# State-space stage of a three-block model: decay sums through DRAM, differential norm inside the groups, merge units behind the last group

## The reference, cut to what matters

```
att = (rms_norm_3(att, subln_w[l], SUBLN_EPS) * (1.0 - lam_init)).reshape(b, s, ATT_V_WIDTH)
ssd = ssd_branch(z, xbc, dt_raw, ...)
merged = sigmoid(gate_a) * (att @ w_branch_attn[l]) + sigmoid(gate_s) * (ssd @ w_branch_ssd[l])
x = x + merged @ w_out[l]
```

```
xbc = silu(causal_depthwise_conv(xbc, conv_w, conv_b))
cum = cumsum(ac);  seg = cum_i - cum_j;  decay = exp(where(causal, seg, -inf))
cb = einsum('bign,bjgn->bgij', cc, bc)
y_diag = einsum('bgij,bgrij,bjgrp->bigrp', cb, decay, xc)
...
y = y * silu(z);  y = y * rsqrt(mean(y*y, per group) + eps) * norm_w
```

## Time and profile before

| | us |
|---|---|
| median of 3 runs (3091.27 to 3093.89) | 3092.34 |
| the profiled execution | 3088.23 |
| its span | 3086.4 |
| TensorE busy in it | 2936.3 (95%) |
| VectorE busy | 925.2 (30%) |
| ScalarE busy | 453.8 (15%) |

### The profile page before, as it was taken

The page is one execution under the profiler, slowest core; times in us unless marked ns, Lnnn a source line. Parts: engine busy times, 40 slices in busy tenths (PEclk is TensorE's granted clock), DMA queues, the critical chain, the costliest instruction groups (busy, mean ns, idle before and its releaser), DMA issues. The chain is left out here.

```text
span 3086.4 us, 33957 instructions
## 1 busy us (share of the span) xinstructions
PE 2936.3 (95%) x14263; PEld 2277.3 (74%) x14263; DVE 925.2 (30%) x1969; ACT 453.8 (15%) x855; POOL 0.2 (0%) x4
## 2 busy tenths in 40 slices
PE   7999999999999999998999999999897899999997
PEld 6888788888887888886888877889786434344343
DVE  2117521021053210532025326455202323222222
ACT  1001410010042100222010012244201010010011
POOL 0000000000000000000000000000000000000000
PEclk9999999999999999998999999899998899999999
DMA  7434144444443443533544443344351899999996
GB/s 241 163 124 163 55 149 151 146 158 146 130 123 116 145 156 122 128 106 82 148 152 148 152 116 91 96 123 116 103 153 43 361 425 427 426 426 427 425 427 257
DMA packets 358885, 590.10 MB, mean 191 GB/s; under 512 B 11376, under 2 KB 315120, under 8 KB 336112
## 3 DMA queue, kind: packets, MB, share of 16 engines
q1 hardware_dynamic: 358064, 586.09, 54.0%
q10 hardware_dynamic: 704, 2.32, 0.2%
HBM read 587.33 MB, written 1.05 MB: 191 GB/s over the span
## 5 line engine op out<-in xcount | busy, mean ns | idle before, releaser
L679 PE MATMUL bank<-hR,ring 128*128 128x256 f32 x3520 | 763.5, 380 | 8.5 <-DVE hR L416 5.6
L679 PEld LDWEIGHTS bank<-hR,ring 128*128 128x128 f32 x3520 | 669.5, 190 | 101.6 <-issue 7.1
L815 PE MATMUL bank<-big,ring 128*128 128x256 f32 x2016 | 440.0, 381 | 4.9 <-ACT big L1013 4.3
L815 PEld LDWEIGHTS bank<-big,ring 128*128 128x128 f32 x2016 | 385.4, 191 | 58.8 <-issue 4.7
L2622 PE MATMUL bank<-ring,wk 128*64 128x512 f32 x1408 | 313.2, 597 | 4.7 <-DMA ring<-in_w_expert_gate 4.7
L2622 PEld LDWEIGHTS bank<-ring,wk 128*64 128x64 f32 x1408 | 99.9, 138 | 211.1 <-issue 211.1
L714 DVE TENSOR_TENSOR wk<-bank,rstd 128x512 f32<-128x512 f32 x88 | 60.9, 692 | 484.3 <-PE bank L679 484.0
L2648 PE MATMUL bank<-big,wk 128*64 128x512 f32 x352 | 155.8, 595 | 15.1 <-ACT wk L2674 15.1
L851 DVE SCALAR_TENSOR_TENSOR xT<-bank,xT 128x512 f32<-128x512 f32 x36 | 24.9, 692 | 454.3 <-PE bank L815 454.3
L2711 DVE TENSOR_TENSOR hT<-bank,hT 128x512 f32<-128x512 f32 x92 | 63.6, 691 | 314.7 <-PE bank L2609 312.4
L1807 PE MATMUL bank<-big,ring 128*128 128x256 f32 x640 | 141.0, 379 | 1.5 <-ACTq L2841 1.0
(11 more groups left out here) (376 smaller groups left out, 2777.7 us busy)
## 6 DMA issues: line engine op xcount, KB each, us to landing
ring<-in_ffn_w_in SPq DMA_DIRECT2D x88, 1024.0 KB
ring<-in_w_expert_gate SPq DMA_DIRECT2D x44, 2048.0 KB
ring<-in_w_expert_up SPq DMA_DIRECT2D x44, 2048.0 KB
ring<-in_w_in SPq DMA_DIRECT2D x96, 512.0 KB
big<-in_w_expert_down SPq DMA_DIRECT2D x44, 1024.0 KB
ring<-in_ffn_w_out SPq DMA_DIRECT2D x20, 2048.0 KB
ring<-in_w_up SPq DMA_DIRECT2D x22, 1024.0 KB
hR<-in_w_expert_down SPq DMA_DIRECT2D x22, 1024.0 KB
```

Source lines behind the costliest of these rows:

```text
L679: last = nc.tensor.matmul(k.bank[:, n % 4, h * S:(h + 1) * S], w[:, c, h * 256 + m * P:h * 256 + (m + 1) * P], k.hR[:, c, :], start=c == 0 ...
L815: return nc.tensor.matmul(k.bank[:, 4 + o // 2, (o % 2) * S:(o % 2 + 1) * S], w[:, c, o * P:(o + 1) * P], self.src[:, n, :], start=n == 0 ...
```

## The change

- The 128 instructions of L2184 are gone. `turn` transposes the cumulative sums (32 heads on 32 partitions) once, between parts of `project_x(0)`; ScalarE copies them out and writes them to a DRAM tensor (`take_rows`); then ScalarE issues, for each head of a group, a transfer that reads the head's row of 1 KB to all 128 partitions (`load_rows`, 4 a group, two groups ahead, into two halves of `hR`). VectorE's differences read that copy in place of the PSUM banks.
- `sums` moves behind `project_x(0)`; `cumulate` and `turn` go between its quarters. `spread` is halved and put behind `project_x(2)` and `project_x(3)`, its `variance`, `root`, `inverse` and `apply` into groups 0, 1 and 2.
- In the last group the merge's unit (0, 0) runs where other groups have `project_x(g+1)`; unit (1, 0) runs ahead of `turn_y(7)`; the units of block 0 and 1 are fetched and used in the order (0,0), (1,0), (0,1), (1,1). Gates and branches change places in the banks.
- `Ssd` loses its barrier; TensorE waits for `yt_taken` instead.

```diff
+        if self.per == 2:
+            self.order[0:4] = [(0, 0), (1, 0), (0, 1), (1, 1)]
...
+    def turn(self, pe):
+        k, nc = self.k, self.k.nc
+        pe.wait_ge(self.tail_ready, 1)
+        for t in range(T):
+            last = nc.tensor.transpose(k.bank[0:32, 7, S + t * P:S + (t + 1) * P], k.sd[:, 4 + t, :], k.c("ident"))
+        last.then_inc(self.rows_turned, 1)
...
+    def take_rows(self, act, chain):
+        act.wait_ge(self.rows_turned, 1)
+        rows = self.k.drow[0:32, 0:S]
+        chain(self.k.nc.scalar.activation(rows, self.k.bank[0:32, 7, S:2 * S], ACT.Copy))
+        act.dma_start(self.k.arg["decay_rows"], rows).then_inc(self.rows_kept, 16)
...
-        self.sub.sums(pe)
-        project_x(0)
-        self.dt.cumulate(pe)
-        self.sub.spread(pe)
-        project_z(0)
-        pe.wait_ge(self.sub.applied, 1)
+        project_x(0, {1: self.dt.cumulate, 2: self.dt.turn})
+        self.sub.sums(pe)
+        project_z(0)
         for g in range(self.G):
-
-            if g:
-                pe.wait_ge(self.seg_done, g)
-            for c in range(T):
-                for r in range(self.R):
-                    last = nc.tensor.matmul(k.bank[:, 5 + c, r * P:(r + 1) * P],
-                                            k.sd[:, 2 + c, 4 * g + r:4 * g + r + 1].to_broadcast([P, P]), k.c("le"),
-                                            start=True, stop=True)
-            last.then_inc(self.cum_bc, 1)
-
             pe.wait_ge(self.conv_silu, g + 1)
...
             if g + 1 < self.G:
                 project_x(g + 1)
+            else:
+                pe.wait_ge(self.sub.applied, 2)
+                pe.wait_ge(self.copied, 2 * self.G)
+                self.merge.unit(pe, 0)
+            if g in (1, 2):
+                self.sub.spread(pe, g - 1)
...
-        pe.wait_ge(self.copied, 2 * self.G)
-        self.fill(pe)
+        pe.wait_ge(self.z_silu, self.G)
+        pe.wait_ge(self.y_summed, self.G)
+        self.merge.unit(pe, 1)
         pe.wait_ge(self.yt_taken, self.G - 1)
         turn_y(self.G - 1)
+        pe.wait_ge(self.yt_taken, self.G)
...
+        def load_rows(g):
+            for r in range(self.R):
+                act.dma_start(self.rows(g, r), self.dt.row(4 * g + r).to_broadcast([P, S])).then_inc(self.rows_loaded[g % 2], 16)
...
         self.sub.square(act, chain)
         self.dt.logs(act, chain)
-        self.sub.root(act, chain)
+        self.dt.take_rows(act, chain)
+        self.dt.decay(act, chain)
+        act.wait_ge(self.dt.rows_kept, 16)
+        load_rows(0)
+        load_rows(1)
         act.wait_ge(self.pads_zero, 1)
         copy_in(0)
-        self.dt.decay(act, chain)
         silu_x(0)
         silu_z(0)
         for g in range(self.G):
...
+            decays(g)
+            if g + 2 < self.G:
+                load_rows(g + 2)
```

More of the change, by code:

```diff
@@ L1814, in gates, with unit @@
             self.part(0, 0, n)
+    def unit(self, pe, j, n0=0):
+        c, u = self.order[j]
+        if n0 == 0:
+            pe.wait_ge(self.loaded(j), self.loads(j))
+        for n in range(n0, len(self.parts(c)[u])):
+            last = self.part(c, u, n)
+        last.then_inc(self.k.w_used, 1)
     def pe(self, pe):
-        k = self.k
         if self.heads:
             pe.wait_ge(self.heads.o_taken, self.heads.at(self.heads.o_taken, self.heads.G))
-        for c in range(KC):
-            if c >= 2:
+            self.unit(pe, 0, 2)
+        for j in range(1 if self.heads else 2, self.UNITS):
+            c, u = self.order[j]
+            if c >= 2 and u == 0:
                 pe.wait_ge(self.merged, self.at(self.merged, c - 1))
[L1823 to L1829, removed]
+            self.unit(pe, j)
     def act(self, act, chain):
@@ L1988, in inverse, with apply @@
         chain(self.k.nc.vector.reciprocal(self.columns(2), self.columns(1)), self.inv_ready)
-    def apply(self, dve):
+    def apply(self, dve, half):
         k, nc = self.k, self.k.nc
[L1992 to L1995, removed]
+        dve.wait_ge(self.spread_ready, half + 1)
+        for b in range(2):
+            a = 16 + 4 * half + 2 * b
+            x = k.big[:, a:a + 2, :]
+            last = nc.vector.scalar_tensor_tensor(x, x, k.ss[:, 14:15], pair(k.bank[:, 5 + b, :]), ALU.mult, ALU.mult)
         last.then_inc(self.applied, 1)
@@ L2083 @@
     UNITS = 16
+    fence = False
     PADW = S + 3
@@ L2308, in per_head, with differences @@
             return k.sd[:, cols, 4 * g:4 * g + 4].rearrange("p t (r d) -> p t r d", d=1).to_broadcast([P, t, self.R, self.D])
[L2310 to L2319, removed]
+        seg = self.w4(self.SEG, 1024)
+        def differences(g):
+            dve.wait_ge(self.rows_loaded[g % 2], 64 * (g // 2 + 1))
             if g:
@@ L2323, in dve @@
                 for r in range(self.R):
-                    last = nc.vector.tensor_scalar(seg[:, c * 512 + r * P:c * 512 + (r + 1) * P], k.bank[:, 5 + c, r * P:(r + 1) * P],
+                    last = nc.vector.tensor_scalar(seg[:, c * 512 + r * P:c * 512 + (r + 1) * P], self.rows(g, r)[:, c * P:(c + 1) * P],
                                                    k.sd[:, 4 + c, 4 * g + r:4 * g + r + 1], 0.0, ALU.subtract, ALU.min)
             chain(last, self.seg_done)
+        self.dt.steps(dve, chain)
+        chain(nc.vector.memset(pad[:, :, 0:3], 0.0), self.pads_zero)
+        self.dt.tail(dve, chain)
+        conv(0)
+        for g in range(self.G):
+            differences(g)
             dve.wait_ge(self.x_taken, g + 1)
```

79 lines of the change are left out of this document (49 added, 30 removed).

## The result

The changed kernel takes 3071.78 us (median, 3071.05 to 3072.62) against 3092.36 beside it: 20.6 us less, a ratio of 0.9933 (95% interval 0.9916 to 0.995). The forecast was 3078.6 with a range of 3073.0 to 3087.0.

What follows compares the result with a forecast made beforehand. TensorE looked like the bound, but in steady groups the chain ending in `y_summed` was nearly as late. Start -5.8, groups -0.3, end -10.2, clock +1.7 and +0.85 gave -13.7 us: 3078.6 against a 3092.34 median, range 3073 to 3087.

Steps and rivals of the forecast that it cites:

- The groups: Steady groups: 15.8 us of TensorE removed, but the wait for `y_summed` takes its place; about -0.3 us in all.
- The 0.85 us for a fall between groups 0 and 1: Gap between groups 0 and 1: 2.0 us idle, one fall of the clock in two, +0.85 us.
- The end: Last group and merge: unit (0, 0) fills the wait for `m_ready`, third block begins earlier; -10.2 us.
- The 1.7 us for the clock: End: idle gaps of about 1.7 and 1.0 us among thin instructions, one fall of the clock counted, +1.7 us.
- The start: From the attention's end to group 0's transposes: 7.5 us earlier, less 1.7 for the clock; -5.8 us.
- The fifth term: Start: half clock behind 2.9 us of TensorE idle ahead of group 0; +1.7 us, bounds 0 and 3.4.
- the clock stays up: Rival for the whole stretch: no fall of the clock anywhere, -18.0 us, 3074.3 us; chance 0.15.
- my own case: The forecast for the whole change, with one to three falls of the clock: -13.7 us, 3078.6 us; chance 0.62.
- Falls in every group: Rival: half clock behind each group's new gap for `y_summed`, -6.1 us, 3086.2 us; chance 0.13.
- Dear issues: Rival: row transfer issues on ScalarE's queue at 1.5 us each cost 19.6 us, so 3098 us; chance 0.05.
- Lost later: Rival: behind the stretch, a later transfer such as router's or experts' weights sets the time; 3086 to 3092 us; chance 0.05.
- the start's bound for the write: Start: the small write to DRAM lands after 1.6 to 4.0 us, taken as 2.2.

Runs made afterwards that it cites:

- experiments 4 to 6: Kernel before with L2184's instructions issued twice, 3101.78 us; one convolution tap left out of the changed kernel, 3000.43 us, and of the kernel before, 3029.51 us.
- after_later_copy: Changed kernel with five copies of 128x512 on ScalarE ahead of `copy_in(0)`; 3075.74 us, ratio 0.9948 against the kernel before.
- no_tail: Changed kernel with the old merge and end (gates alone in the last group, old unit order, barrier); 3080.02 us, ratio 0.9969 against the kernel before.
- rows_only: Kernel before with only the decay sums through DRAM, norm and end as before, transposition behind `spread`; 3103.49 us, ratio 1.0041.
- rows_early: Kernel before with only the decay sums through DRAM, norm and end as before, transposition inside `project_x(0)`; 3096.35 us, ratio 1.0013.

## Why the prediction was right in its mechanisms and wrong in its size

*The groups.* Right, and shown: 15.8 us of TensorE were removed and the groups gained 0.7, because `y_summed` was 0.2 us behind (experiments 4 to 6). A steady group gained 0.20 and not 0.10. The transposes' weight load follows `y_summed` by 0.07 us, where I had allowed 0.11. And the periods run between matmuls, where the distance fell from 0.32 us (2045.49 to 2045.81) to 0.10 (2093.08 to 2093.18). Groups 1 and 2 came at 26.29 and 26.26, against 26.28 and 26.26 before and 0.07 more forecast. The differences, which I had taken as equal, read SBUF in 1.66 us for eight instructions and had read PSUM in 2.16; it lies in the room ahead of `m_ready`, of which 1.5 us and more were left in every group but the last, where 0.5 was. The 0.85 us for a fall between groups 0 and 1 was not paid in any of the profiles of the changed kernel; the idle there is 1.9 us.

*The end.* Right: 10.7 against 10.2. The 1.7 us for the clock is the right size for an event that comes in some executions, three of seven.

*The start.* This is the step that failed, by its size: I forecast TensorE idle for 2.9 us ahead of group 0 and half clock behind it, a gain of 5.8; it was 10.0. The mechanism stood (`copy_in(0)` is queued on ScalarE behind the write and eight issues, and `silu_x` is the later one), but four sizes were off. In this profile half clock lasted 1.6 us into `project_x(0)`, where the forecast took over the 5.1 us of before, so against the end of the attention `sums` began 2.2 us earlier than forecast. The write landed in 1.5 us, hidden by `decay`, while the issues took 0.63 us and not 0.47: `copy_in(0)` came 1.0 us earlier than forecast. From there to the end of `silu_x` it took 8.8 us and not 10.1, since the table load of 1.28 us, which before stood behind the convolution, with `decay` between the copy and silu, now runs under it. Sum 2.5 us with 0.2 of rest. And the clock fell behind `sums` already, which delayed `project_z(0)` by 1.8 us and so ate the idle that I had counted. The fifth term, 1.7 us for half clock on the path, was therefore not due; `after_later_copy` shows that at 3.5 us of idle it would have been, at that price.

The rival "the clock stays up", 3074.3, was the nearest: 18.0 forecast, 18.9 and 20.6 measured. I gave it 0.15 and my own case 0.62, and of the falls that my case counted none stood on the path in the first profile of the changed kernel, and one in the second. But a wrong count of falls alone does not leave the range, as 3074.3 lies inside it. What does is the start's chain, 30.7 us in my sum and 28.35 in the profile: 18.0, with 2.5 for it, 0.5 for the end and 0.4 for the groups, is the 21.4 of the profiles. Half clock that ended early is the largest of its four sizes. In `no_tail` it ended 2.5 us later, `sums` began 1.2 us later, and the start took 29.4. So part of what exceeded the forecast is luck of the execution, and no term of my sum had a range for it. Before's own scatter is in the timed difference as well: its medians were 3089.2 to 3092.4 over the comparisons, and the first was the highest.

*The other rivals.* My reason against the first, that every gap of over 2.4 us ended at half clock, is nearly so: three of them (at 20, 358 and 962 us) ended at full clock, and the fall came 0.3, 0.7 and 0.0 us later. Falls in every group: none behind the 1.4 us gaps in the profiles of the changed kernel. In `no_tail`, `rows_only` and `rows_early` half clock did follow group 7's transposes, but there 9.5 us of idle stand behind them. Dear issues: 0.33 to 0.48 us each in the groups, 0.63 at the start with weights in flight, far from 1.5 (by that rival's own formula the gain would be gone at 1.3, not 1.2). Lost later: 752.7 and 752.1 us, nothing lost. The row transfers landed in 2.9 us (median). The first eight, beside the weights, took 3.0 to 8.5; group 0's last row was there at 1984.30, 3 us ahead of its differences at 1987.35, so they held nothing up, as the prediction had it. My sentence on the start's bound for the write, 1.6 to 4.0, held in neither direction: 1.5 here, 4.5 in `rows_only`. On this the Trainium skill ("DMA: Bandwidth & Descriptors", section "Anatomy of one DMA — SWDGE (gpsimd) path") says that the fixed part of a transfer issued by GpSimd is about 2 us and mostly the confirmation of the write, which can be surprisingly long with HBM as the target. The write here is issued by ScalarE, for which that section gives no figure: its 1.5 us in the changed kernel lie a little below 2, and the 4.5 in `rows_only` are the long kind that it warns of.

What stays open: why half clock ended at such different times after the attention (1.6 to 1.8 us in seven profiles of the changed start, 4.2 in two, 12.1 to 14.5 with `sums` ahead of `project_x(0)`); why the write took 2.8 us in `rows_early`; what the moved norm gives without the transfers; and whether the end's fall can be provoked or avoided other than by closing the gap.

## What to carry to other kernels

Before instructions of the busiest engine are removed, subtract the times of the two latest arrivals at the next wait: what is won is their difference, here 0.2 us of 1.97, and the waits view does not show it because the wait is covered. A freed resource can be worth more than the freed time: the bank that the removal left unused gave 12 us, the removal itself under 1. A round trip through DRAM must not have critical work queued behind its wait; by its place the same edit cost 13 us or 4. A possible fall of the clock is a term with a chance, so it belongs in the range more than in the sum.

## What the runs showed of the hardware that I had not expected

- Half clock stood behind 3.7 us of one-column matmuls at full rate, though TensorE had no idle time: `project_z(0)` took 8.84 us in place of 7.07 in all eight profiles in which it follows `sums` at once.
- A gap of about 2.1 us among thin instructions was followed by half clock in three of seven profiles with the same instructions, and cost 1.7 us each time; gaps of 1.4 and 1.9 us with 7 us of dense matmuls ahead were not, and one of 3.5 us was.
- A write of 32 KB to DRAM landed after 1.5 us in the changed kernel, after 2.8 us in `rows_early`, in both with next to nothing else in flight (about 20 GB/s), and after 4.5 us in `rows_only`, there with weights arriving at 217 GB/s.
